# Attention scores of a hybrid encoder layer: a projection product ahead of each unit's score products and one between its two heads

## What is computed

```python
qr = q row, in blocks of 16 columns                     # (b, h, 4 blocks, 16, 64)
kr = 8 rows x 32 columns of keys around each block
s = jnp.einsum('bhnqd,bhrnkd->bhnqrk', qr, kr)          # the scores
s = jnp.where(colmask_b, s + bias, -1e30)
p = jax.nn.softmax(s over the 8 * 32 keys)
o = jnp.einsum('bhnqrk,bhrnkd->bhnqd', p, vr)
```

## Time and profile before

| | us |
|---|---|
| median of 3 runs | 1434.45 |
| the runs, lowest and highest | 1433.8, 1434.76 |
| the profiled execution, its own time | 1432.91 |
| its span, first to last instruction | 1431.1 |
| PE busy | 1385.4 |
| PEld busy | 1139.7 |
| DVE busy | 788.2 |
| POOL busy | 479.7 |
| ACT busy | 441.7 |

### The profile page before, as it was taken

The page is one execution under the profiler, slowest core; times in us unless marked ns, Lnnn a source line. Parts: engine busy times, 40 slices in busy tenths (PEclk is TensorE's granted clock), DMA queues, the critical chain, the costliest instruction groups (busy, mean ns, idle before and its releaser), DMA issues.

```text
span 1431.1 us, 18721 instructions
## 1 busy us (share of the span) xinstructions
PE 1385.4 (97%) x6959; PEld 1139.7 (80%) x6959; DVE 788.2 (55%) x1346; ACT 441.7 (31%) x924; POOL 479.7 (34%) x219
## 2 busy tenths in 40 slices
PE   7999999999999998899999999999999999999998
PEld 4877777888888887788788888888888888888886
DVE  4343456878968789525744434434434444226657
ACT  4233336437264272511422122122122122212210
POOL 3322231211122121135634334334433434544460
PEclk9999999999999999999999999999999999999999
DMA  8100210210201102143311111111111115111112
GB/s 253 45 31 30 89 31 29 50 45 21 73 32 39 56 17 52 42 147 118 118 45 45 58 44 44 59 44 44 46 57 44 44 59 191 44 44 59 44 59 103
DMA packets 49799, 89.25 MB, mean 62 GB/s; under 512 B 24464, under 2 KB 27216, under 8 KB 49488
## 3 DMA queue, kind: packets, MB, share of 16 engines
q1 hardware_dynamic: 44848, 71.46, 15.9%
q10 hardware_dynamic: 4896, 17.04, 3.2%
HBM read 77.71 MB, written 10.78 MB: 62 GB/s over the span
## 4 chain that ended last, share of the span: by engine, by line
PE 38%; issue 37%; DVE 12%; POOL 10%; ACT 1%; DMA 1%; POOLq 1%; SPq 0%; DVEq 0%; ACTq 0%
PE banks L647 11%; POOL w_hi L531 8%; PE banks L622 6%; PE banks L964 6%; PE banks L1064 3%; DVE qkv L1632 1%; PE banks L756 1%; PE banks L781 1%; DVE d_n L1815 1%; PE banks L769 1%; DVE inv L1727 1%; DVE outer L1724 1%; PE banks L932 1%; PE banks L940 1%; DVE u_t L1828 1%
## 5 line engine op out<-in xcount | busy, mean ns | idle before, releaser
L531 POOL TENSOR_TENSOR w_hi<-w_raw,one 128x1024 fp32r<-128x1024 f32 (+1 forms) x99 | 187.5, 1894 | 876.2 <-PE banks L622 291.4
L622 PE MATMUL banks<-x_hi,w_hi 128*128 128x512 f32 (+1 forms) x912 | 358.6, 393 | 12.0 <-POOL w_lo L534 8.6
L622 PE MATMUL banks<-x_hi,w_lo 128*128 128x512 f32 (+1 forms) x912 | 355.8, 390 | 0.0
L622 PE MATMUL banks<-x_lo,w_hi 128*128 128x512 f32 (+1 forms) x912 | 355.6, 390 | 0.0
L1940 DVE SCALAR_TENSOR_TENSOR cv<-banks,fw,cv 128x511 f32<-128x511 f32 x176 | 131.9, 750 | 261.7 <-ACT cv L1455 254.0
L534 POOL TENSOR_TENSOR w_lo<-w_raw,w_hi 128x1024 fp32r<-128x1024 f32 (+1 forms) x99 | 251.4, 2540 | 7.8
L622 PEld LDWEIGHTS banks<-x_hi,w_hi 128*128 128x128 f32 (+1 forms) x912 | 170.7, 187 | 49.6 <-POOL w_lo L534 8.6
L622 PEld LDWEIGHTS banks<-x_hi,w_lo 128*128 128x128 f32 (+1 forms) x912 | 170.6, 187 | 37.0 <-issue 0.6
L622 PEld LDWEIGHTS banks<-x_lo,w_hi 128*128 128x128 f32 (+1 forms) x912 | 170.7, 187 | 36.8 <-issue 1.1
L1455 ACT ACTIVATE cv<-banks,fw_j 128x512 f32<-128x512 f32 x88 | 68.7, 780 | 337.1 <-PE banks L622 334.7
L1969 DVE TENSOR_TENSOR a_lo<-act,a_hi 128x1024 fp32r<-128x1024 f32 x39 | 65.0, 1673 | 96.6 <-ACT a_hi L1473 96.5
(11 more groups left out here) (212 smaller groups left out, 1955.9 us busy)
## 6 DMA issues: line engine op xcount, KB each, us to landing
w_raw<-w_all SPq DMA_DIRECT2D x102, 512.0 KB, 3.3
mix<-decay_dram SPq DMA_DIRECT2D x8, 512.0 KB, 4.4
z_tok<-x_tok ACTq DMA_DIRECT2D x8, 512.0 KB, 5.8
x_dram<-z_tok ACTq DMA_DIRECT2D x8, 512.0 KB, 2.6
z<-x_dram ACTq DMA_DIRECT2D x8, 512.0 KB, 8.4
y<-z SPq DMA_DIRECT2D x7, 512.0 KB, 2.6
mix<-xT SPq DMA_DIRECT2D x12, 256.0 KB, 9.0
gb<-ln_row ACTq DMA_DIRECT2D x4, 512.0 KB, 8.4
```

Source lines behind the costliest of these rows:

```text
L531: nc.gpsimd.tensor_tensor(w_hi[u][:, 0:n], w_raw[ru][:, 0:n], one[:, :].to_broadcast([P, n]), ALU.mult).then_inc(w_high, 1)
L622: last = mm(ps[bank][0:cols, :], w[u][:, k * cols:(k + 1) * cols], seq(x[:, k, :], s), start=n == 0, stop=n == 3 * KT - 1)
```

## The change

`scores` now takes the filler and issues one projection product before its waits and one more between the two heads' products. To keep the number of projection products per step, the `fill(per)` that follows becomes `fill(per - 2)` in the eight steps that have scores. Lines after the edit shift: the score product is L762, the transposes L775 and the value products L787 in the changed kernel.

```diff
-                scores(pair, 0)
-                fill(per)
-                scores(pair, 1)
+                scores(pair, 0, fill)
+                fill(per - 2)
+                scores(pair, 1, fill)
                 turn_values(pair, 0)
                 turn_values(pair, 1)
-                fill(per)
+                fill(per - 2)
...
                     if n < UNITS:
-                        scores(pair, n)
-                    fill(per)
+                        scores(pair, n, fill)
+                        fill(per - 2)
+                    else:
+                        fill(per)
...
-            def scores(pair, n):
+            def scores(pair, n, fill):
+
+                fill(1)
                 s, b = unit(n)
...
                     pe.wait_ge(s_biased, 8 * pair + n)
                 for h in range(2):
+                    if h:
+                        fill(1)
```

## The result

| | before | after |
|---|---|---|
| median of 5 runs, us | 1434.68 | 1463.15 |
| lowest and highest | 1433.8, 1437.06 | 1461.24, 1465.36 |
| the profiled execution, its own time | 1432.91 | 1463.15 |
| its span | 1431.1 | 1461.4 |

The change makes the kernel slower: a ratio of 1.0197, 95% interval 1.0184 to 1.0209. The medians differ by 28.5 us, the two profiled executions by 30.2 us; the forecast was 31.1 us and 1465.5.

A forecast was written before the change was run, and what follows sets the result against it. TensorE's own time was taken to bound the kernel. 26.6 us for parted heads, 4.0 for leading projections and 0.5 of wait sum to 31.1 us, moving the median from 1434.45 to 1465.5 us, range 1458 to 1472.

The forecast's parts named there:

- What bounds the kernel: Whole kernel: TensorE's own time is the time, busy 1385.4 of 1431.1 us; nothing in the attention stage hides added PE time.
- A head alone costs what both cost, 0.63 us: Score block: the two heads run side by side, so one head parted from the other still takes 0.63 us.
- One more entry, 0.09, and one more first projection, 0.11: Around the parted heads: each unit pays 0.09 us more to empty the array and 0.11 us more uncovered load.
- 32 units at 0.83, 26.6 us: Projection between the heads: 8 units in each of 4 pairs, each 0.83 us longer, 26.6 us in all.
- 20 leading places at 0.20, 4.0 us: Projection ahead of head 0: where a narrow block stood ahead, 0.20 us at each of 20 places, 4.0 us.
- The wait for `v_tok`, 0.5 us: Last pair: TensorE waits 0.5 us more for v_tok, with two projections fewer behind the scores.
- No new wait for `s_biased`: Last pair, between units 0 and 1: TensorE has 1.75 us against 1.44 needed, so no added wait.
- Nothing hidden later: Behind the attention stage: everything starts later by the sum, and waits there move but do not shrink.
- Rival C: PE's idle time elsewhere absorbs the 31.1 us and the time stays at 1434.5; 1% for within 0.2%.
- Rival A, loads pulled ahead: Loads of head 1's block and the projections hide across the shape change: 21.8 us slower, 1456.3; 5%.
- the 16.3 us of "issue" idle: Weight loader idles around the scores, 6.3 us ahead and 10.0 behind: the price of changing block shape, not fillable stalls.

The follow-up runs named there:

- same_half: Kernel before, with head 1's score product reading head 0's partitions, so both need the same half of the array; 1448.47 us, ratio 1.0095, stage +13.5 us.
- mid_only: Changed kernel with only the projection between the heads kept, none ahead of head 0; 1458.13 us, ratio 1.0166 against the kernel before, stage +26.2 us.
- lead_only: Changed kernel with only the projection ahead of head 0 kept, none between the heads; 1436.38 us, ratio 1.0024 against the kernel before, stage +3.9 us.
- same_half_after: Changed kernel, with head 1's score product reading head 0's partitions; 1464.14 us in one run, stage 210.34 us against the changed kernel's 210.35.
- mid_two: Changed kernel with two projections between the heads instead of one; 1462.80 us, ratio 1.0211 against the kernel before, stage 210.9 us.
- two_units_even: Kernel before, with scores, turns and values by two units, evenly spaced, ACT evacuating one projection earlier; last pair only scores by two; 1428.78 us, ratio 0.9966.

## Why the prediction was right

- **What bounds the kernel.** TensorE, everywhere in the stage. The 30.25 us that it lost there came out in the end to within 0.1 us (spans: 30.3).
- **A head alone costs what both cost, 0.63 us.** This was a bound that I had to choose, from 265-column products of another shape. Measured 0.63 in the changed kernel, and by its complement, 0.42 us more for a pair that may not share, in same_half.
- **One more entry, 0.09, and one more first projection, 0.11.** The lone projection takes 0.42 where the sum said 0.23 + 0.09 + 0.11 = 0.43.
- **32 units at 0.83, 26.6 us.** mid_only: 26.2, with 0.2 of wait in it. So a unit costs 0.81, and the forecast was 0.6 too high here.
- **20 leading places at 0.20, 4.0 us.** lead_only: 3.9, with 0.2 of wait for `v_tok` in it (1.26 against 1.03). So the places cost 3.7: 19 at 0.19, and the twentieth nothing.
- **The wait for `v_tok`, 0.5 us.** 1.5 against 1.0.
- **No new wait for `s_biased`.** In the last pair unit 1's scores start 1.75 us after head 1 of unit 0, as worked out from projections and blocks alone, so the 0.4 us that the view of waits puts down to DVE is the loader's usual idle at a change of shape by another name (0.35 us behind a run of projections): DVE's addition, which raises `s_biased`, ended at 236.63, 0.26 us before the scores started. In the timelines of PE and DVE:

```profile
235.14 0.70 PE L762 MATMUL banks<-k_nat,q_nat 64*128 64x256 f32 x2
...
236.89 0.70 PE L762 MATMUL banks<-k_nat,q_nat 64*128 64x256 f32 x2
...
235.94 0.69 DVE L1598 TENSOR_TENSOR s_sb<-banks,bm 128x512 f32<-128x512 f32 x1 [1.47 <-PE banks L762]
```

- **Nothing hidden later.** 1189.85 and 1190.15 us behind the stage. Rival C is out. That the two lie within the 1 us that the prediction allowed is luck: in the ten profiled executions this part takes from 1188.3 to 1193.1 us with the same instructions.
- **Rival A, loads pulled ahead.** Out: the loads ahead of all 64 blocks of scores, and of the projections behind them, start with their product, and same_half_after equals the changed kernel. Of the two rules of the Trainium skill weighed there, the one on draining at a change of tiling mode ("TensorEngine Tiling (Array Packing)", Key Properties) agrees with the trace, which shows the next start 0.09 us late there; that this is emptying is a reading, as no run takes the 0.09 apart. The one on loads pulled ahead ("TensorE: Matmul & The Clock Gate", on what happens when a matmul is issued) agrees inside a shape, where same_half's second records follow without their load, but not across a change of shape.
- **What was off, the idle of the loader.** The prediction calls the 16.3 us of "issue" idle the price of the changes of shape. That price is read from TensorE's starts: 32 visits at 0.09 and 0.11 are 6.4 us at most, and the rest of the idle costs nothing. Nor is 0.35 us the usual idle ahead of scores. In the kernel before, 27 of the 32 are 0.17 us, behind transposes and value products, and the five of 0.32 to 0.37 add the rest of the 6.3. In the changed kernel every block of scores stands behind a projection, 60 of them behind a lone one whose own load came late, and there the idle is 0.24 to 0.25. So the sum went from 6.3 to 15.6 us and did not just double, at no cost to TensorE.
The forecast was 31.1 us for the profiled execution and it was 30.2; the 0.9 are the 0.6 and the 0.3 above. The median moved by 28.5. The 1.7 us between these two are within the spread of the part behind the stage, seen next.

## What to carry to other kernels

Small products that sit side by side in different halves of TensorE's array are one block: whatever full-size product is put between them pays for both halves one after the other and for another change of shape, here 0.81 us a time. Before filling an idle of the weight loader with other work, compare the starts of the products around it. If the load starts with its product and the shape changes there, the idle comes with the change: its price is what the starts are late, not the idle's length, and the cure is to change shape less often (here 4.8 us by putting two units' scores together), as long as the chain that feeds the next step has the time it had.

## What the runs showed of the hardware

A change of shape costs about the same wherever a projection or a score block stands next to it: 0.09 us more to the first score record from the projection ahead, and an uncovered load of about 0.11, for the first projection behind a 64*128 or 128*64 block (0.33 and 0.34 for 0.23) as for the first score record (0.32 for 0.21).

I had not expected the part behind the stage to vary by itself. In lead_only it took 1193.0 us, in mid_only 1192.9, in mid_two 1188.3, against 1189.85 in the kernel before, with the same instructions. The windows of lead_only during the first LayerNorm show one of the causes:

```profile
716.00:721.60 5.60, 3.67 (x21) 2.91 (x20) 1.37 (x3) 1.74 (x4) 3.62 (x2) 1.00 0.36 123
...
721.60:725.00 3.40, 3.40 (x10) 2.64 (x9) 1.50 (x2) 0.31 (x1) 0.00 (x0) 0.50 0.31 113
726.00:729.40 3.40, 3.40 (x16) 2.79 (x16) 0.73 (x1) 1.52 (x2) 0.00 (x0) 1.00 0.00 0
```

In the second of the three TensorE ran at 1.2 GHz, though it was busy all the time, and handled 10 products where 16 went in the third at 2.4 GHz. Ahead of it, it had been busy for 3.67 of 5.60 us and had waited 1.9 us for DVE; the kernel before has 3.84 of 5.60 at the same place and kept its clock. The stretch from the first transposes of the LayerNorm to the down projection took 510.2 us in this execution and in the three others with such a piece (mid_only, same_half, two_units_even), and 508.5 to 508.6 in the six without. Two to five more such pieces stand in each execution between 550 and 625 us, in the DeltaNet heads; one of the changed kernel, with what TensorE did ahead of it:

```profile
585.00:588.40 3.40, 1.43 (x13) 1.46 (x14) 3.26 (x8) 1.22 (x5) 0.00 (x0) 1.00 0.41 163
588.40:591.80 3.40, 3.40 (x19) 3.40 (x17) 3.37 (x7) 0.91 (x2) 0.00 (x0) 0.50 0.02 5
```

TensorE had been busy for 1.43 of 3.40 us at full clock, with one idle of 2.8 us that began before, and then ran the next stretch at half. From the stage to the output projection the executions differ by up to 4.8 us (361.8 to 366.6), least with two such pieces and most with five; the parts behind it, the LayerNorm stretch above left out, agree within 0.1 us. The other runs of the kernel before say the same: of 46 further runs of the kernel before, the 19 with a mean granted clock of 0.997 or more took 1430.8 to 1432.6 us, and the 20 with 0.994 or less 1433.8 to 1436.7. Why the pieces come in one execution and not in the next was not tried. They are one reason why a difference of under 2 us between medians says little for this kernel, and why the stage's length in the profile was the better measure of each edit: it came out as 210.35 and 210.34 us in the changed kernel and in same_half_after.
